# A hybrid decoder layer on one Trainium2 core: probabilities scaled on ScalarE, negated maxima, and a first expert gather in feature halves

## The reference

```python
x_n = rmsnorm(h, norm_mix_g)
q_sb, k_sb, v_sb, q_mb, k_mb, v_mb, g_sb, g_mb = split(x_n @ w_in)
y_sb = stick_breaking_attention(q_sb, k_sb, v_sb)          # 8 heads of 64
y_mb = softmax(q_mb k_mb / 8 + rel_bias, causal) @ v_mb     # 8 heads of 64
h = h + (sigmoid(g_sb) * (y_sb @ w_proj_sb) + sigmoid(g_mb) * (y_mb @ w_proj_moba)) @ w_out
hn = rmsnorm(h, norm_ffn_g)
logits = hn @ w_router + b_router
top_w = softmax(top_4(logits))
for e in range(32):
    gate, up = split(hn @ w_gate_up[e] + b_gate_up[e])
    y = ((clip(up) + 1) * gate * sigmoid(1.702 * gate)) @ w_down[e] + b_down[e]
    h = h + gates[:, e] * y
out = rmsnorm(h, norm_final_g)
```

## Time and profile before

| | |
|---|---|
| median of three runs | 1134.88 us (1134.66 to 1135.31) |
| profiled execution | 1134.32 us, of which the span 1132.6 us |
| TensorE busy | 1073.5 us (95%) |
| VectorE, ScalarE, GpSimd busy | 259.9, 151.1, 122.2 us (23%, 13%, 11%) |
| moved by DMA | 437.3 MB, 386 GB/s in the mean |
| chain that ended last, by engine | TensorE 56%, DMA 40%, VectorE 2% |
| expert 0's first gate/up matmul | 227.64 us |

### The profile page before, as it was taken

One profiled execution on the slowest core, in us unless ns is written; L12 is line 12 of the kernel. 1 busy time (PEld: TensorE's weight loads), 2 busy tenths in 40 slices (PEclk: granted clock), 3 DMA queues, 4 the chain that ended last, 5 costly groups with the idle time before them and its releaser, 6 DMA issues.

```text
span 1132.6 us, 14442 instructions
## 1 busy us (share of the span) xinstructions
PE 1073.5 (95%) x6022; PEld 451.5 (40%) x6022; DVE 259.9 (23%) x482; ACT 151.1 (13%) x315; POOL 122.2 (11%) x140
## 2 busy tenths in 40 slices
PE   8999999999999999999999999999999999999986
PEld 7676444633434333333333333333333333333322
DVE  2345756621111111111111112111210111111112
ACT  2233222320000000000000001000100000000002
POOL 1357592400000000000000000000000000000000
PEclk9999999999999999999999999999999999999999
DMA  9943238899999999999999999999999999999996
GB/s 321 346 184 150 88 136 352 353 370 428 426 428 435 427 428 428 431 429 432 429 432 435 428 429 435 427 429 433 434 428 429 432 433 428 432 426 428 426 424 255
DMA packets 36705, 437.30 MB, mean 386 GB/s; under 512 B 4488, under 2 KB 5568, under 8 KB 16992
## 3 DMA queue, kind: packets, MB, share of 16 engines
q1 hardware_dynamic: 34752, 435.44, 91.5%
q10 hardware_dynamic: 1920, 1.39, 0.5%
HBM read 435.76 MB, written 1.06 MB: 386 GB/s over the span
## 4 chain that ended last, share of the span: by engine, by line
PE 56%; DMA 40%; DVE 2%; issue 1%; ACT 0%; SPq 0%; POOL 0%; POOLq 0%
DMA ring<-in_w_down_dram 29%; PE bank L1905 19%; PE bank L1942 13%; DMA ring<-in_w_gate_up_dram 11%; PE bank L1583 9%; PE bank L1567 5%; PE bank L1878 2%; PE bank L1872 2%; PE bank L1933 1%; PE bank L1667 1%; PE bank L1893 0%; PE bank L1927 0%; PE bank L1692 0%; DMA resid<-in_x_dram 0%; PE bank L1527 0%
## 5 line engine op out<-in xcount | busy, mean ns | idle before, releaser
L1905 PE MATMUL bank<-ring,gates 128*64 128x512 f32 x2048 | 472.2, 604 | 16.8 <-DMA ring<-in_w_gate_up_dram 16.8
L1942 PE MATMUL bank<-ring,gates 128*64 128x512 f32 x1008 | 225.5, 595 | 26.1 <-DMA ring<-in_w_down_dram 25.9
L1905 PEld LDWEIGHTS bank<-ring,gates 128*64 128x64 f32 x2048 | 139.2, 138 | 261.8 <-issue 230.8
L1415 DVE TENSOR_SCALAR gates<-bank 128x512 f32<-128x512 f32 x31 | 21.4, 692 | 709.4 <-PE bank L1905 709.4
L1942 PEld LDWEIGHTS bank<-ring,gates 128*64 128x64 f32 x1008 | 71.1, 137 | 175.5 <-issue 140.2
L709 POOL COPY expert_sel<-expert_row 96x64 bf16 x32 | 7.5, 233 | 843.7 <-PE bank L1872 838.1
L619 POOL TENSOR_TENSOR ring<-ring 128x512 f32<-128x512 f32 x60 | 82.6, 1409 | 67.0 <-DVE ring L1072 34.9
L1872 PEld LDWEIGHTS bank<-onehot,qkT 128*128 128x128 bf16 x1488 | 52.2, 118 | 25.2 <-issue 25.2
L1878 PE MATMUL bank<-gates,scatter_w 64*128 64x512 f32 x248 | 61.6, 615 | 0.0
L929 ACT ACTIVATE gates<-gates 128x512 f32<-128x512 f32 x32 | 20.2, 630 | 279.4 <-DVE gates L1415 279.2
L1872 PE MATMUL bank<-onehot,qkT 128*128 128x64 bf16 x1488 | 55.5, 198 | 0.0
(11 more groups left out here) (257 smaller groups left out, 646.9 us busy)
## 6 DMA issues: line engine op xcount, KB each, us to landing
ring<-in_w_gate_up_dram SPq DMA_DIRECT2D x44, 4096.0 KB, 28.1
ring<-in_w_down_dram SPq DMA_DIRECT2D x59, 2048.0 KB, 21.1
ring<-in_w_gate_up_dram SPq DMA_DIRECT2D x39, 2048.0 KB, 14.4
ring<-in_w_in_dram SPq DMA_DIRECT2D x9, 2048.0 KB, 15.4
ring<-in_w_down_dram SPq DMA_DIRECT2D x7, 1024.0 KB, 25.4
ring<-in_w_out_dram SPq DMA_DIRECT2D x2, 2048.0 KB, 8.7
ring<-in_w_in_dram SPq DMA_DIRECT2D x4, 512.0 KB, 7.3
ring<-in_w_proj_sb_dram SPq DMA_DIRECT2D x1, 2048.0 KB, 7.9
```

The source lines that it names most:

```text
L1415: V.tensor_scalar(gate_t, bank[4][:, :], SWIGLU_LIMIT, None, ALU.min).then_inc(gate_rd, 1)
L1905: ins = mm(bank[4 + i][SLOTS * c:SLOTS * (c + 1), :], xe[:, k, :], ring[:, base + k // 2, n0:n0 + CH], start=False, stop=k == KD - 1)
L1942: ins = mm(bank[to][SLOTS * c:SLOTS * (c + 1), :], rows, ring[:, place, j * D + c * CH:j * D + (c + 1) * CH], start=k == 0, stop=k == KD - 1)
```

## The change

- In `biased_scores` the maxima are written negated by the reduction itself, into `nmx`; the separate negation goes. `score_rd` is signalled for each of the two row blocks, and ScalarE's Exp waits for its own block only.
- `even_weights` only takes the reciprocals; ScalarE multiplies the probabilities, behind its four Exps of the pair.
- GpSimd writes the third bf16 piece of tile 0 itself, and the selector of expert 0 right after it; ScalarE's copy of it goes.
- The residual is copied to all four banks on ScalarE, the copies placed between those of tile 1's pieces; the load of `b_down` comes behind them.
- `first_gather` works in feature halves, into banks 7 and 6, and VectorE multiplies by the gains in halves (`first_tokens`); expert 0's bias matmuls wait for the selector only. The rank sums move from bank 2 to bank 6, the dummy matmuls of `keep_clock` to bank 7.
- The negation of the top logits moves from `choose` to `count`, for both tiles at once. Some semaphores are merged.

```diff
@@ ScalarE, softmax pairs
                     for b in range(2):
-                        act.wait_ge(score_rd, 2 * (p - SB_PAIRS) + b + 1)
                         for q, (c0, c1) in enumerate(((0, P), (P, TRI))):
+                            act.wait_ge(score_rd, 2 * (2 * (p - SB_PAIRS) + b) + q + 1)
                             nc.scalar.activation(att_s[:, b, c0:c1], att_s[:, b, c0:c1], ACT.Exp,
                                                  bias=nmx[:, b, q:q + 1], accum_out=rs[:, b, q:q + 1]
                                                  ).then_inc(prob_raw, 1)
+                    for b in range(2):
+                        act.wait_ge(even_rd, 2 * (p - SB_PAIRS) + b + 1)
+                        for q, (c0, c1) in enumerate(((0, P), (P, TRI))):
+                            nc.scalar.activation(att_s[:, b, c0:c1], att_s[:, b, c0:c1], ACT.Copy,
+                                                 scale=rr[:, b, q:q + 1]).then_inc(prob_rd, 1)
@@ VectorE, biased_scores and even_weights
-                    V.reduce_max(mx[:, b, 0:1], att_s[:, b, 0:P], AX_X)
-                    link(V.reduce_max(mx[:, b, 1:2], att_s[:, b, P:TRI], AX_X))
-                    V.tensor_scalar(nmx[:, b, :], mx[:, b, :], -1.0, None, ALU.mult).then_inc(score_rd, 1)
+                    V.tensor_reduce(nmx[:, b, 0:1], att_s[:, b, 0:P], AX_X, ALU.max, negate=True).then_inc(score_rd, 1)
+                    V.tensor_reduce(nmx[:, b, 1:2], att_s[:, b, P:TRI], AX_X, ALU.max, negate=True).then_inc(score_rd, 1)
...
-                    link(V.reciprocal(rr[:, b, :], rs[:, b, :]))
-                    for q, (c0, c1) in enumerate(((0, P), (P, TRI))):
-                        V.tensor_scalar(att_s[:, b, c0:c1], att_s[:, b, c0:c1], rr[:, b, q:q + 1], None, ALU.mult
-                                        ).then_inc(prob_rd, 1)
+                    V.reciprocal(rr[:, b, :], rs[:, b, :]).then_inc(even_rd, 1)
@@ GpSimd, tile 0's third piece and the first selector
-            left_over(1, 0, slice(0, D), 2)
+            pool.wait_ge(piece_rd, 2)
+            nc.gpsimd.tensor_tensor(pieces[2][:, 0, :], res2[0], pieces[1][:, 0, :], ALU.subtract).then_inc(third_p, 1)
+            nc.gpsimd.tensor_copy(expert_sel[:, :], expert_row[:, 0:1].to_broadcast([3 * E, SLOTS])).then_inc(sel_rd, 1)
@@ ScalarE, before the experts
             root(1)
-            next_piece(2, 0, slice(0, D), left_p, 2)
             first_piece(1, low)
             first_piece(1, high)
+            start_rows(0, 1)
             next_piece(1, 1, low, left_d, 1)
+            start_rows(3, 2)
             next_piece(1, 1, high, left_d, 2)
-            start_rows(0, 1)
-            start_rows(3, 2)
-            act.wait_ge(piece_rd, 7)
+            start_rows(2, 3)
+            start_rows(1, 4)
+            act.wait_ge(third_p, 1)
             act.dma_start(bdown_sb, b_down[0]).then_inc(late_in, 16)
-            start_rows(1, 4)
-            act.wait_ge(routed, NT)
+            act.wait_ge(top_rd, 1)
@@ VectorE, before the experts
-                V.tensor_scalar(stat[:, 16 + t:17 + t], top[:, t, 0:1], -1.0, None, ALU.mult)
...
             def count():
-                link(V.reduce_max(cnt_f[:, :], bank[2][:, NT * E:NT * E + E], AX_X))
+                V.tensor_scalar(stat[:, 16:18], top[:, :, 0:1].rearrange("p t o -> p (t o)"), -1.0, None, ALU.mult
+                                ).then_inc(top_rd, 1)
+                link(V.reduce_max(cnt_f[:, :], bank[6][:, T + NT * E:T + NT * E + E], AX_X))
...
+            def first_tokens(h, at, ready, done):
+                dve.wait_ge(ready, 1)
+                V.tensor_tensor(xeT[:, 4 * h:4 * h + 4, :], at[:, 0:T].rearrange("p (k s) -> p k s", k=4),
+                                gslot[:, h, :].rearrange("p (r o) -> p r o", o=1).to_broadcast([P, 4, SLOTS]), ALU.mult
+                                ).then_inc(done, 1)
...
                 if r is None:
-                    left_over(1, 5)
-                    third_piece(0, 6)
-                    third_piece(1, 7)
-                next_tokens(0, done)
-                if r is None:
+                    left_over(1, 4)
+                    third_piece(0, 5)
+                    third_piece(1, 6)
+                    first_tokens(0, bank[7], gathered_low, xe_low)
+                    first_tokens(1, bank[6], gathered, xe_rd)
                     count()
-                    start_rows(2)
@@ TensorE, first gather and first gate/up
+                for h in range(2):
+                    tokens(0, 0, h, piece_rd, 1)
+                    tokens(0, 1, h, piece_rd, 2)
+                    tokens(0, 2, h, third_p, 1)
+                    tokens(1, 0, h, piece_rd, 3 + h)
+                    tokens(1, 1, h, piece_rd, 5 + h)
+                tokens(1, 2, 0, third_rd, 1).then_inc(gathered_low, 1)
+                ins = tokens(1, 2, 1, third_rd, 2)
                 ins.then_inc(gathered, 1)
...
                     if ahead:
-                        pe.wait_ge(xe_rd, g + 1)
+                        pe.wait_ge(xe_low, 1)
                 for k in ks:
+                    if k == 4 and isinstance(g, int) and g == 0:
+                        pe.wait_ge(xe_rd, 1)
```

More of the change, by code:

```diff
@@ L704, in _, with experts @@
             left_over(0, 0, slice(0, D), 1)
-            left_over(1, 0, slice(0, D), 2)
-            def experts(done):
-                with pool.Fori(0, E) as e:
+            pool.wait_ge(piece_rd, 2)
+            nc.gpsimd.tensor_tensor(pieces[2][:, 0, :], res2[0], pieces[1][:, 0, :], ALU.subtract).then_inc(third_p, 1)
+            nc.gpsimd.tensor_copy(expert_sel[:, :], expert_row[:, 0:1].to_broadcast([3 * E, SLOTS])).then_inc(sel_rd, 1)
+            def experts(done, start=0):
+                with pool.Fori(start, E) as e:
                     pool.wait_ge(gathered, e + (done + 1))
@@ L710, in experts @@
                                           ).then_inc(sel_rd, 1)
-            experts(0)
+            experts(0, 1)
             more_passes(pool, lambda r: experts(r * E), most_tokens(pool))
@@ L1388, in weigh @@
                 return most_tokens(dve)
-            def start_rows(n):
-                V.tensor_copy(bank[n][:, :], resid[:, n // 2, n % 2 * CH:(n % 2 + 1) * CH]).then_inc(start_rd, 1)
             def one_hots(col):
@@ L1543, in mean_row @@
                     ins = mm(bank[6][:, t * P:(t + 1) * P], neg_one[:, :], diag[t], start=True, stop=True)
-                ins.then_inc(rrow_ps, 1)
+                ins.then_inc(start_ps, 1)
             def bias_rows():
                 pe.wait_ge(u_in, 32)
-                mm(bank[7][0:HMB, 0:UW], rel_sb[:, :], hot_sb[:, :], start=True, stop=True).then_inc(u_ps, 1)
+                mm(bank[7][0:HMB, 0:UW], rel_sb[:, :], hot_sb[:, :], start=True, stop=True).then_inc(start_ps, 1)
             def unit(u):
@@ L1790, in keep_clock @@
                 for _ in range(times):
[L1791 removed]
+                    mm(bank[7][:, 0:T], ident[:, :], slot_no[:, :, :], start=True, stop=True)
             def open_rows(n):
[L1795 to L1796 removed]
+                c0 = (E, E, 0, 0)[n]
+                mm(bank[n][:, c0:CH], ones_bf[0:3 * E, :], bgu[:, c0:CH], start=n >= 2, stop=True,
                    skip_group_check=True).then_inc(open_ps, 1)
@@ L1832, in _ @@
             pe.wait_ge(routed, 1)
-            pe.wait_ge(consts2, 3)
-            rk = bank[2]
+            pe.wait_ge(consts, 6)
+            rk = bank[6][:, T:CH]
             mm(rk[:, 0:E], before[:, :], selb[:, 0, :], start=True, stop=True)
@@ L1853, in first_gather, with tokens @@
                 pe.wait_ge(onehot_rd, 1)
-                low, high = range(KD // 2), range(KD // 2, KD)
-                steps = [(0, 0, range(KD), 1), (0, 1, range(KD), 2), (0, 2, range(KD), 3), (1, 0, low, 4),
-                         (1, 0, high, 5), (1, 1, low, 6), (1, 1, high, 7), (1, 2, low, 1), (1, 2, high, 2)]
-                for t, i, ks, ready in steps:
-                    pe.wait_ge(piece_rd if t == 0 or i < 2 else third_rd, ready)
-                    for k in ks:
-                        ins = mm(bank[7][:, k * SLOTS:(k + 1) * SLOTS], pieces[i][:, t, 4 * P * (k // 4) + k % 4:4 * P * (k // 4 + 1):4],
-                                 onehot[:, t, :], start=t == i == k == 0, stop=t == NT - 1 and i == 2,
-                                 skip_group_check=True)
+                def tokens(t, i, h, ready, n):
+                    pe.wait_ge(ready, n)
+                    for k in range(4 * h, 4 * h + 4):
+                        ins = mm(bank[7 - h][:, k % 4 * SLOTS:(k % 4 + 1) * SLOTS], pieces[i][:, t, 4 * P * h + k % 4:4 * P * (h + 1):4],
+                                 onehot[:, t, :], start=t == i == k % 4 == 0, stop=t == NT - 1 and i == 2,
+                                 skip_group_check=True)
+                    return ins
+                for h in range(2):
[6 more added lines that the diff above has]
+                ins = tokens(1, 2, 1, third_rd, 2)
                 ins.then_inc(gathered, 1)
```

37 lines of the change are left out of this document (19 added, 18 removed).

## The result

The changed kernel takes 1136.85 us, the median of 14 runs (1133.19 to 1139.52), against 1134.55 for the kernel before beside it (14 runs, 1133.87 to 1135.31). The ratio is 1.002, with a 95% interval of 1.0012 to 1.0029: slower, by 1.4 to 3.3 us, where the forecast was 2.8 us faster. The runs also lie wider apart than before's. The profiled execution took 1134.78 us, its span 1133.0; it is the second quickest of the 14, so its trace shows the mechanism but not the whole difference of the medians.

What follows compares the result with a forecast made beforehand. The DMA weight stream was taken as the bound, its start setting the end: 1.3 + 1.8 us earlier, less 0.3, gives 2.8 us. Profiled 1131.5 us, median 0.56 higher: 1132.1 us, range 1131.0 to 1134.1.

Steps and rivals of the forecast that it cites:

- Attention, the gaps: Attention: TensorE's two waits on `last_rows`, 1.04 and about 0.25 us, close, making TensorE 1.3 us earlier.
- Attention, the cover: Attention: scalings queued on ScalarE delay nothing; cost nothing, with 1.7 us of cover before `keep_first` is needed.
- Rival 2: Attention part gives nothing: negating reduction waits for GpSimd, or VectorE's sums before pair 5 come later; 1133.4 us, 13%.
- The slower rival that I gave, the clock: TensorE's clock falls in expert 0 while the stream depends on TensorE; about 1142 us, 7%.
- (a): Before the experts: top-logit negation moves from `choose` to `count`; 0.1 us credited, the later softmax wait costs nothing.
- (b): Before the experts: GpSimd writes the bf16 piece, ScalarE loses a 1.04 us copy; costs nothing, over 2 us of cover.
- (c): Before the experts: residual copies on ScalarE end sooner, so the `resid` load is issued 1.8 us earlier.
- (d): Before the experts: early selector and halved gains multiplication let expert 0 start on TensorE 0.6 us sooner.
- (e): Before the experts: `b_down`'s load now comes behind the copies and competes with the stream, losing 0.3 us.
- The stream against TensorE: Start of the expert loop: the stream gains 0.9 us on TensorE without running dry; cover 2.5 us, 0.4 at the bound.
- Rival 1: TensorE paces the stream, which runs dry before the fifth load; 1133.0 us at worst, 14%.

Runs made afterwards that it cites:

- neg_only_late: Changed kernel with the scalings back on VectorE, negated maxima kept, and bank 2's residual copy on VectorE, so the `resid` load comes later: 1131.66 us, ratio 0.997.
- yield_late: `yield` with bank 2's residual copy back on VectorE, so the load into `resid` is issued 1.5 us later: 1131.64 us, ratio 0.9975.
- no_att_late: `no_att` with bank 2's residual copy back on VectorE, so the load into `resid` is issued later: 1133.63 us, ratio 0.9988.
- late_bd_late: `yield_late` with the load of `b_down` issued after the first step of expert 0, into the running stream: 1132.55 us, ratio 0.9982.
- yield: Changed kernel with GpSimd waiting for the blocked VectorE sum between its two groups of sums: 1132.86 us, ratio 0.9982.
- no_att: Changed kernel with its attention part undone, negation and scaling on VectorE again: 1134.44 us, ratio 0.9999.
- before_step2: Kernel before, with the VectorE sum moved by about 0.87 us through three small reductions ahead of it: 1134.74 us, ratio 1.0000.
- yield_half: `yield` with the load into `resid` issued only after the first step of expert 0: 1132.71 us, ratio 0.9984.

## Why the prediction was wrong

- **Attention, the gaps.** Right, and undersized: at 162 us TensorE had gained 1.82 us in this part, forecast 1.3. I took the gaps at their idle time, 1.04 and 0.25 us; they were worth 1.30 and 0.51, each 0.26 more, as at the new wait above. The closing of the second I gave to the scalings; `neg_only_late`, with the scalings back, has neither gap. Without the lock-out the part is worth as much on the medians: 2.84 us in `yield_late` less 1.07 in `no_att_late` is 1.77. The reduction cost 0.29 us, and four scalings on ScalarE 1.48 us (forecast 1.4); nothing waited for them.
- **Attention, the cover.** This step failed: the move of the scalings was to cost nothing. I took every operation that left VectorE as time gained, and asked only what it had delayed ahead of `last_rows`. I had the earlier trace rows with the 2.39 us, and read them as a price only. I did not go on to the VectorE operations with two SBUF inputs behind pair 7, which meet the same run of GpSimd. The price was 3.06 us at TensorE, where the part had gained 1.82.
- **Rival 2** named GpSimd, but ahead of pair 5 and for a microsecond. It stood at 1133.4; nothing in my list ended at +2.3 through VectorE. The slower rival that I gave, the clock, didn't come: the granted clock is 1.00 in all the rows of after above. The 0.91 of 320 to 340 us in the earlier trace rows is 1.00 in after, with no effect on the end.
- **(a), (b).** Right. GpSimd's subtraction with a bf16 output took 2.14 us, as its fp32 form did (2.13 in the earlier trace rows).
- **(c).** Right in place, wrong in worth: counted from 207 us the load was issued 1.94 us earlier, forecast 1.8. The end did not follow.
- **(d).** Right: counted from 207 us expert 0 gained 0.77 us, forecast 0.6, and this is what the end follows.
- **(e).** Wrong in its premise: the issue stands at 225.57, ahead of the two copies that it follows in the program, so `b_down` stayed out of the stream. The size for a load inside the stream was too low: 0.9 us in `late_bd_late`, where I had 0.3 by bytes.
- **The stream against TensorE.** This is the second step that failed: the end was to move with the stream's start, and it moves with expert 0. Rival 1 held, at 14%. I had 2.5 us of cover by the rate of the 1 MB pieces in before, and 0.4 at the bound of 430 GB/s. The stream was to gain 0.9 us on TensorE, so at that bound the cover was already too small by 0.5, which I didn't say. The loads between are no reserve either: two of them wait for TensorE (229.60 and 231.32 us above). In the kernel after the stretch from 232 us shows 418 GB/s, so the bound was the nearer end, and the stream is thin at 234 us already (213 GB/s). Taken by expert 0 alone, my sum would have been 1.3 + 0.6 = 1.9 us; by what the runs show, 1.8 and about 1.

Without the lock-out the change gains 1.6 us on the median (`yield`). With the late load, which the change doesn't have, it gains 2.84, just what I had forecast; that is chance, since it comes by expert 0, with the load into `resid` issued 1.06 us behind it.

The Trainium skill, "SBUF — State Buffer", section "Who interferes with whom", says that a VectorE instruction with two SBUF inputs contends with a GpSimd instruction that reads SBUF, and that a `tensor_reduce` never does. The traces agree: 9.57 us for the one, 0.29 us for the other. The Trainium skill, "SBUF — State Buffer", section "SBUF: two separate sides", says of such a pair that whichever "starts first gets the pair for the whole instruction"; by that, as an estimate, the sum would have waited for the rest of one GpSimd operation of 1.23 us. In these traces it stood through more than seven of them, and there the measurement decides. The rule of the Trainium skill that I cited ahead, "Perfetto Trace Analysis", section "Optimizing Scalar/DVE Operations", sees a use in offloading where VectorE is saturated. VectorE was 23% busy, and the move cost 3.7 to 4.2 us, so the traces bear the rule out, though for another reason than VectorE's speed.

What stays open:

- What makes the sum be kept out. In nine traces with the scalings on ScalarE and no pause it stands 8.3 to 9.8 us; in five with them on VectorE (`before`, `no_att`, `no_att_late`, `before_step2`, `neg_only_late`), 0.65 to 1.05 us. A reading that fits these is that VectorE gets in if a larger operation of its own has competed less than about 7 us before: the scalings end at about 159 us in before and at 156.5 in `neg_only_late`. No run puts a small operation at that distance, or leaves the large ones only at a greater one, so size and time aren't told apart. But in the kernel after another sum gets in at 120.18 us in 1.45 us, after 11 us of GpSimd's run without such an operation. So the reading is incomplete, and the decision is not explained.
- Why the early load costs 1.0 to 1.4 us. That the stream runs thin behind it is seen; that this is the cause is only argued. `yield_half`, with a load later still, is slower than `yield_late`, so it is not simply "the later the better".
- Why after's runs spread over 6 us, and part of its loss. Both of its traces show the long sum, but both are of quick runs (the second of 14 and the first of 8). In the first, expert 0 starts 0.04 us behind before's and the run takes 0.46 us more; the median takes 2.3 us more. The cost of the early load may be part of the rest; that isn't shown.

## What to carry to other kernels

Before moving an operation off an engine, ask what its presence did for the order of others: here a slow, waiting VectorE operation kept a later one from being locked out, and the move turned 2.4 us of cheap waiting into 9.6 us of expensive waiting. Look for every operation with two SBUF inputs that will meet a gapless GpSimd run, on the far side of the edit too, and if there is one, let GpSimd wait for it once: here that wait cost GpSimd 0.4 us and brought 4. The better repair here was to leave the scalings where they were, since their move had gained nothing. When a transfer stream and an engine both start late, move one without the other on the chip before crediting the gain to either.

## What the runs showed of the hardware that I had not expected

- A VectorE sum of 0.42 us stood 8.3 to 9.8 us, in nine traces, beside GpSimd sums of 1.23 us; where GpSimd waited for it between two of its sums, it ended 0.28 us behind the first, and reductions of 128x128 beside the same run kept their 0.29 us.
- A 128x2 operation of 0.48 us, over 10 us ahead of the sum, did not change this; scalings of 128x128 and 128x256 that ended 5.7 to 6.5 us ahead of it did.
- A DMA issue that follows two activations in ScalarE's program started ahead of both (225.57 against 226.10 us).
- A load of 128 KB put into the full stream cost 0.9 us on the median, three times its bytes at 430 GB/s.
- A product of TensorE behind a wait lost 0.26 us more than the idle time that the profile shows, at both of before's waits (modelled ends).
